# Four transformer layers on one core: setup reordered and partly moved into the first mixer, and the order of weight and modulation loads at the end of two up projections

## What is computed

```python
def first_block(x, ...):
    h = x
    for l in range(2):
        n = rms_norm(h, attn_norm[l])
        h = h + (hybrid_mixer(n, ...) if l == 0 else diff_mixer(n, ...))
        h = h + conv_glu_ffn(rms_norm(h, ffn_norm[l]), ffn_w_up[l], ffn_conv_w[l], ffn_conv_b[l], ffn_w_down[l])
    return rms_norm(h, final_norm)

def second_block(x, c, ctx, c_ctx, ada_w, ada_b, ...):
    for l in range(2):
        mod_l = split(silu(c) @ ada_w[l] + ada_b[l], 6)       # six rows of 1024 that modulate the tokens
        mod_c = split(silu(c_ctx) @ ada_w[l] + ada_b[l], 6)   # and six for the 256 context tokens
        ...                                                   # mixer and feed-forward, modulated and gated
```

## Time and profile before

| what | us |
|---|---|
| three timed executions | 2000.79, 2011.51 (median), 2018.67 |
| the profiled execution, own time | 1996.9 |
| its span, first to last instruction | 1995.1 |
| PE busy in the span | 1800.3 (90%) |
| mean granted TensorE clock | 0.948 of full speed |
| POOL busy | 935.9 (47%) |
| ACT busy | 878.3 (44%) |
| DVE busy | 721.8 (36%) |

### The profile page before, as it was taken

The page is one execution under the profiler, slowest core; times in us unless marked ns, Lnnn a source line. Parts: engine busy times, 40 slices in busy tenths (PEclk is TensorE's granted clock), DMA queues, the critical chain, the costliest instruction groups (busy, mean ns, idle before and its releaser), DMA issues.

```text
span 1995.1 us, 25840 instructions
## 1 busy us (share of the span) xinstructions
PE 1800.3 (90%) x10191; PEld 1453.6 (73%) x10191; DVE 721.8 (36%) x1591; ACT 878.3 (44%) x1541; POOL 935.9 (47%) x408
## 2 busy tenths in 40 slices
PE   2898999989879989798888998999999798889998
PEld 2666887776568878687554577888878686759986
DVE  2244232235432222337266524443401253344431
ACT  3455543435554433342334534444432255456652
POOL 2654674766346657343203023444444161137876
PEclk9999999999889999898885898999999999999999
DMA  4434998444249984232100022333323431125654
GB/s 168 150 97 137 301 306 297 162 150 136 66 147 307 305 296 154 80 100 70 64 1 1 1 63 66 104 98 92 106 74 105 105 106 43 43 85 153 186 171 146
DMA packets 257258, 261.36 MB, mean 131 GB/s; under 512 B 11107, under 2 KB 201667, under 8 KB 250867
## 3 DMA queue, kind: packets, MB, share of 16 engines
q1 hardware_dynamic: 256019, 255.10, 40.4%
q10 hardware_dynamic: 1120, 4.63, 0.6%
HBM read 258.66 MB, written 1.05 MB: 130 GB/s over the span
## 4 chain that ended last, share of the span: by engine, by line
PE 77%; DVE 8%; ACT 5%; DMA 4%; issue 2%; SPq 1%; POOL 1%; DVEq 0%; ACTq 0%
PE bank L341 21%; PE bank L342 20%; PE bank L343 20%; PE bank L1371 2%; PE bank L710 2%; PE bank L1022 2%; PE bank L733 2%; ACT weights_high L328 2%; DMA weights<-in_ffn_w_down 1%; ACT work L1140 1%; PE bank L992 1%; PE bank L1722 1%; PE bank L396 1%; PE bank L718 1%; SPq L2460 1%
## 5 line engine op out<-in xcount | busy, mean ns | idle before, releaser
L335 POOL TENSOR_TENSOR weights_low<-weights,weights_high 128x1024 fp32r<-128x1024 f32 (+1 forms) x388 | 917.3, 2381 | 954.4 <-ACT weights_high L328 954.1
L328 ACT ACTIVATE weights_high<-weights 128x1024 fp32r<-128x1024 f32 (+1 forms) x388 | 400.8, 1045 | 485.4 <-PE bank L343 143.1
L341 PE MATMUL bank<-normed_features_high,weights_high 128*128 128x256 f32 (+1 forms) x1408 | 444.6, 316 | 13.4 <-DVE normed_features_low L447 6.7
L342 PE MATMUL bank<-normed_features_high,weights_low 128*128 128x256 f32 (+1 forms) x1408 | 439.1, 312 | 0.0
L343 PE MATMUL bank<-normed_features_low,weights_high 128*128 128x256 f32 (+1 forms) x1408 | 438.7, 312 | 0.0
L341 PEld LDWEIGHTS bank<-normed_features_high,weights_high 128*128 128x128 f32 x1408 | 271.8, 193 | 65.6 <-issue 34.5
L341 PE MATMUL bank<-weights_high,normed_features_high 128*128 128x512 f32 (+4 forms) x752 | 291.5, 388 | 26.4 <-DVE normed_features_low L488 9.2
L342 PEld LDWEIGHTS bank<-normed_features_high,weights_low 128*128 128x128 f32 x1408 | 272.0, 193 | 13.8
L343 PEld LDWEIGHTS bank<-normed_features_low,weights_high 128*128 128x128 f32 x1408 | 271.8, 193 | 14.0
L343 PE MATMUL bank<-weights_low,normed_features_high 128*128 128x512 f32 (+4 forms) x752 | 276.4, 368 | 0.0
L342 PE MATMUL bank<-weights_high,normed_features_low 128*128 128x512 f32 (+4 forms) x752 | 276.3, 367 | 0.0
(11 more groups left out here) (289 smaller groups left out, 2026.2 us busy)
## 6 DMA issues: line engine op xcount, KB each, us to landing
work<-in_ada_w SPq DMA_DIRECT2D x48, 1024.0 KB, 8.0
weights<-in_ffn_w_up SPq DMA_DIRECT2D x44, 1024.0 KB, 6.3
weights<-in_ffn_up SPq DMA_DIRECT2D x44, 1024.0 KB, 6.0
weights<-in_ffn_w_down SPq DMA_DIRECT2D x20, 1024.0 KB, 5.1
weights<-in_ffn_down SPq DMA_DIRECT2D x20, 1024.0 KB, 5.0
weights<-in_diff_w_qkv SPq DMA_DIRECT2D x12, 1024.0 KB, 5.1
weights<-in_hyb_w_in SPq DMA_DIRECT2D x11, 1024.0 KB, 5.3
weights<-in_odd_w_in SPq DMA_DIRECT2D x9, 1024.0 KB, 5.3
```

Of the source, the lines that this page charges most:

```text
L328: A.eng.activation(high(whigh[:, m % HIGHS, :]), raw(wslot[:, u % SLOTS, :]), ACT.Copy).then_inc(scalar_done, A.one(("A", "high", m)))
L335: G.eng.tensor_tensor(raw(wlow[:, u % SLOTS, :]), raw(wslot[:, u % SLOTS, :]), high(whigh[:, m % HIGHS, :]).bitcast(F32), ALU.subtract).th ...
L341: T.eng.matmul(out_, lh, rh, start=first, stop=False)
L342: T.eng.matmul(out_, ll, rh, start=False, stop=False)
```

## The change

**Setup.** ACT issues the identity alone (64 KB) and the tokens `x`. SP issues weight slot 0, the gains of the first norm, weight slots 1 and 2, then everything else (25 small loads, the rest of `con` among them) and last the context tokens. A new first phase (`first_T`, `first_V`, `first_A`) turns the unscaled tokens, turns the first gains, sets the small constants, loads the square-root table, and computes the squares of the two token tiles. The first norm now has the form of `front_T`, `front_V` and `front_A`; the high parts of the first four halves are made between its features. The rest of the setup goes into the mixer: `setup_T` into cut 1 behind its second half, `setup_V` behind DVE's reads of cut 0, `setup_lambda_V` and `setup_A` behind cut 2. In `setup_A` stand an Exp, a Silu, a copy and the four squares of the context tiles.

**End of the up projections of block one.** The list `issue` now has tiles 20 and 21, the first down weights, tile 22, the second, tile 23, the third. `down_T` waits only for the first modulation rows; it uses banks 7 and 4 for the left half, the modulation columns are turned in the right half before its ninth chunk, and DVE adds the first two parts of the residual ahead of the modulation columns.

```diff
-                    issue.extend(("ada", first + n) for n in ([0, 1] if f == 2 else [f - 1] if f < FC - 1 else range(f - 1, ADA_N)))
+                    issue.extend(("ada", first + n) for n in ([0, 1] if f == 2 else [f - 1] if f < FC - 1 else [f - 1, f]))
-        def add_down_halves(ph, w):
+        def add_down_halves(ph, w, ada=()):
             begin(ph)
+            left = list(ada)
...
                     issue.append(("weights", len(stream) - 1))
+                    if left:
+                        issue.append(("ada", left.pop(0)))
...
-        add_down_halves("1.0 ffn down", io["ffn_w_down"][0])
+        add_down_halves("1.0 ffn down", io["ffn_w_down"][0], [ADA_N - 2, ADA_N - 1])
...
         def front_T(T, ph, x_ph):
 
-            turn_x_T(T, ph, x_ph, 1)
+            if x_ph != "setup":
+                turn_x_T(T, ph, x_ph, 1)
...
-                if k % 4 == 3:
+                if x_ph == "setup" and k in (0, 2, 4, 6):
+                    ahead(A, first_half[next_ph] + 1 + k // 2)
+                if x_ph != "setup" and k % 4 == 3:
                     ahead(A, first_half[next_ph] + HIGHS - 1 + k // 4)
...
-        DOWN_BANKS = {"1.0 ffn down": (2, 3, 0, 1), "1.1 ffn down": (2, 3, 0, 1), "2.0 ffn down": (4, 5, 6, 7, 0, 1, 2, 3), "2.1 ffn down": (0, 1, 6, 7)}
+        DOWN_BANKS = {"1.0 ffn down": (7, 4, 0, 1), "1.1 ffn down": (7, 4, 0, 1), "2.0 ffn down": (4, 5, 6, 7, 0, 1, 2, 3), "2.1 ffn down": (0, 1, 6, 7)}
...
-            last = FC - 3 if n > SEQ or up in WITH_ADA else FC - 2
-            T.eng.wait_ge(vector_done, done("V", up, "low", last))
+            if up in WITH_ADA:
+                T.eng.wait_ge(vector_done, done("V", up, "rows", 0))
...
-                    if half == 0 and f0 == 12 and middle is not None:
+                    if half == 1 and f0 == 8 and middle is not None:
                         middle(T)
...
+        def first_T(T):
+            T.eng.wait_ge(ident_in, 16)
+            T.eng.wait_ge(x_in, 16)
+            for half in range(2):
+                for j, t in enumerate(LAT):
+                    for k in range(4 * half, 4 * half + 4):
+                        i = T.eng.transpose(turned_k(k)[:, j * P:(j + 1) * P], xt[:, t, k * P:(k + 1) * P], ident)
+            i.then_inc(tensor_done, T.one(("T", "1.0 norm", "turned")))
+            T.eng.wait_ge(first_in, 16)
+            T.eng.transpose(psum[0][:, 0:16], vrows[0:16, :], const("ident", 0, 16, slice(0, 16))).then_inc(tensor_done, T.one(("T", "setup", "gains")))
...
+        def first_A(A):
+            A.eng.wait_ge(vector_done, done("V", "setup", "eps"))
+            A.eng.activation(stat[:, 32:33], lam[:, 6:7], ACT.Sqrt).then_inc(scalar_done, A.one())
+            A.eng.wait_ge(x_in, 16)
+            for t in LAT:
...
         def setup_A(A):
-            A.eng.wait_ge(x_in, 16 * 2)
...
+            A.eng.wait_ge(vector_done, done("V", "setup", "cols"))
             A.eng.activation(lam[:, 2:4], lam[:, 0:2], ACT.Exp).then_inc(scalar_done, A.one(("A", "setup", "exps")))
...
+            A.eng.wait_ge(ctx_in, 16)
+            for t in CTX:
+                for half in range(2):
...
-              between={(1, 2, 1): [fox_T]}, after_V={1: [fox_V]}, after_A={1: [fox_A]}, following="1.0 norm2")
+              between={(1, 1, 1): [setup_T], (1, 2, 1): [fox_T]}, after_V={0: [setup_V], 1: [fox_V], 2: [setup_lambda_V]}, after_A={1: [fox_A], 2: [setup_A]}, mixed="setup", following="1.0 norm2")
...
-                if what == "weights" and u == 2:
-
-                    for dst, src in loads[N_LOADS // 3:]:
-                        sp.dma_start(dst, src).then_inc(loaded, 16)
...
+                if u == 0:
+                    sp.dma_start(vrows[0:16, :], rows(io["attn_norm"].rearrange("a n -> (a n)"))).then_inc(first_in, 16)
+                if u == SLOTS - 1:
+                    for dst, src in loads:
+                        sp.dma_start(dst, src).then_inc(loaded, 16)
+                    sp.dma_start(xt[:, 0:2, :], io["ctx_2"][0].rearrange("(t p) d -> p t d", p=P)).then_inc(ctx_in, 16)
```

73 lines of the change are left out of this document (35 added, 38 removed).

## The result

| | before | changed |
|---|---|---|
| median of five timed runs, us | 2006.53 (2000.79 to 2018.67) | 1990.12 (1989.35 to 1990.46) |
| ratio of the changed kernel to before | | 0.9909, 95% interval 0.9886 to 0.9932 |
| profiled execution, us (span, mean granted clock) | 1996.9 (1995.1, 0.948) | 1989.65 (1987.9, 0.942) |
| PE's first product, us | 42.56 | 21.86 |
| fourth weight slot issued, us | 50.68 | 37.89 |

The change brings 16.4 us between the medians, where 28.4 were forecast, and 7.2 us between the two profiled executions. Two different things are missing: some 10 us are missing in the first 38 us of the changed kernel, and the profiled execution of before turns out to be a quick one of its program.

The account below looks back on a forecast made before the run. PE, carrying 77% of the chain, was taken to bound the kernel. Start and mixer (23.2 - 1.0 - 1.5 = 20.7 us) plus transitions (7.7) gave 28.4, so 2011.5 - 28.4 = 1983.1 us; range 1966 to 1999.

Parts of the forecast that it names:

- Beside them PE turns the tokens: Start: tokens land at 7.9 us, PE transposes them beside ACT's squares until 11.6, first product at 19.2.
- Cut 0 needs two halves ... so I keep 8.1.: First mix: cut 0 takes 8.1 us as before, its features being ready, so slot 0 is free at 27.3.
- SP must also be there by then.: Start: SP's queue, with ten more issues, is through at 25 or 26 us; mixer anchored at 27.5, saving 23.2.
- The rival of SP's queue: Start: small loads ahead of the fourth weight slot make PE wait in cut 1; slower, chance 0.05.
- The mixer, 1.0 for the transposes and 1.5 for `setup_A`: Mixer: setup work moved there costs the path 1.0 us for seven small transposes and 1.5 for ACT's `setup_A`.
- the longer price weighed in the prediction: ACT's table loads: a skill page adds a drain of about 1.38 us per switch, making `setup_A` 9.4 us; not used.
- The transitions, 2.4 + 2.3 + 3.0 = 7.7: Block one, up to down: 2.4 and 2.3 us from shorter waits in two layers, 1.5 each from regained clock.
- I take the saving over to the median unchanged.: Saving summed on the profiled execution, 1996.9 us, is subtracted whole from the timed median, 2011.51.
- nothing at the transitions: Block one, up to down: PE swaps one wait for another, clock falls the same; saves 20.7, time 1990.8, chance 0.13.
- 20.7 us for the start: Start and mixer together: 23.2 us saved at the anchor, less 1.0 and 1.5 charged in the mixer.
- ACT's new work is on the path: Mixer: all 6.6 us of `setup_A` delay PE, plus 1.7 at half clock; saves 16, time 1995.5, chance 0.12.

Follow-up runs that it names:

- experiment 11: Changed kernel with features in PSUM, bias loads early, gains turned ahead of tokens, two high parts moved, weight slots 1 and 2 behind nine small loads; 1981.45 us.
- experiment 3: Changed kernel with the first norm's features written to two PSUM banks instead of SBUF; 1983.64 us, ratio 0.9866.
- experiment 4: Changed kernel with ACT making the high parts of the first four weight halves before the features; 1982.5 us, ratio 0.987.
- 9: Changed kernel with first four high parts ahead of the features, features in PSUM, bias loads early, context squares early; 1981.62 us, ratio 0.9855.
- 12: Kernel of experiment 11 with both remaining modulation tiles of each block-one layer behind the first down weights; 1971.59 us, ratio 0.9805.
- experiment 2: Kernel before with only the new step from up to down projection in block one, old setup kept; 2001.87 us, ratio 0.9963.
- experiment 1: Changed kernel with the step from up to down projection in block one as before, so only the new setup; 1990.28 us, ratio 0.9908.

## Why the forecast was near and its sum was not

The time, 1990.1, lies in the range (1966 to 1999) and 7.0 us above the forecast of 1983.1. Point by point:

- **"Beside them PE turns the tokens", the tokens at 7.9, the first product at 19.2.** Right in kind, 2.7 us late. The tokens landed at 9.6 (8.4 us from issue, not 6.6; experiment 11 excludes weight slots 1 and 2 as the reason, which stays open). Then ACT waited 1.31 us, until 13.91, for a small operation that stands on DVE behind the turned gains, which PE turned last, at 13.31; the sum had the roots wait for the squares alone.
- **"Cut 0 needs two halves ... so I keep 8.1."** This is the step that failed, with its premise that the features "will be ready now". It took 16.0 us, 4.5 of them waits for DVE's low parts. The sum asked which engine makes each operand, and not whether two engines can work at once: the change moved POOL's subtractions beside DVE's, and each DVE subtraction with two SBUF inputs waited for one of POOL's. With the cause taken away, cut 0 took 7.4 us (experiment 3) and 8.9 (experiment 4), around the 8.1. So the term was right for a kernel without the collision, and 7.9 us were missing.
- **"SP must also be there by then."** Right: SP was through at 21.1, earlier than the 25 or 26 forecast. The rival of SP's queue can be dropped; it came true only in experiments 9, 11 and 12, where the bias loads were put there.
- **The mixer, 1.0 for the transposes and 1.5 for `setup_A`.** The 12.8 us at the fourth slot were 12.4 at the first slot of `hyb_w_out`, near the mixer's end (132.46 before, 120.02 changed): 0.4 against the 2.5 charged. Another 1.5 went between there and `ffn_w_up`, 38.6 us before and 40.1 in the changed kernel; but the second profile of before took 40.1 too, and all fourteen lie at 38.4 to 38.7 or at 40.0 to 40.2. In the 5 us that begin 15 us into this part the granted clock was 1.00 in the first profile of before and 0.74 in the changed kernel. `setup_A` took 6.3 us, forecast 6.6; ACT's rows of its head stand below. Its two table loads took 1.28 us each, the next activation begins 0.01 us behind each, and the first load begins 0.02 us behind the activations ahead of it (59.11 and 3.88 are 62.99). So the longer price weighed in the prediction is not seen here either.

```profile
59.11 3.88 ACT L334 ACTIVATE weights_high<-weights 128x1024 fp32r<-128x1024 f32 x4
63.01 1.28 ACT L1932 ACT_TABLE_LOAD   x1
64.30 0.20 ACT L1932 ACTIVATE lam<-lam 128x2 f32<-128x2 f32 x1
64.53 1.28 ACT L1933 ACT_TABLE_LOAD   x1
65.82 0.22 ACT L1933 ACTIVATE st<-veccol 128x16 f32<-128x16 f32 x1
```

- **The transitions, 2.4 + 2.3 + 3.0 = 7.7.** Measured 6.0 in the changed kernel and 8.6 alone, and some 4 over all profiles (experiment 2), so the term was rather too large. The mechanism is the one named: the wait for DVE is exchanged for one for tile 23 behind the second down weights. The sum charged 2.8 us for the megabyte ahead of it; taking that megabyte away brought 5.2 us in the first layer and 2.3 in the second (each from the layer's first up slot to the first slot of the projection that follows; between experiments 11 and 12 the same edit brought 3.0 and 3.9), with the clock that comes with it.
- **"I take the saving over to the median unchanged."** This held better than what the two profiles show. The profiled pair is only 7.2 us apart, because the profile of before is a quick execution: a second one took 2007.6, against which the changed kernel is 19.7 us faster. At the entry to block two the gain is 17.0 or 21.0 us by the two profiles, and by the medians it is 16.4 to 20.3.

The rival "nothing at the transitions" gave this very time, 1990.8, from 20.7 us for the start, of which 11 to 12 arrived, and from no gain at the transitions, which experiment 2 excludes for block one (by experiment 1 most of that gain is lost again in block two, with one more slow round of its recurrent stage). "ACT's new work is on the path" (1995.5) falls with the changed kernel itself: between the fourth slot and `ffn_w_up` 1.8 us are lost, not the 9.3 that this rival adds up. That the forecast is only 7.0 us off has a part of luck: the sum was 12.0 too high against the medians, 10.4 of it at the fourth slot (37.89 where 27.5 was forecast), and 5.0 came back only since the kernel before measured 2006.5 in five runs and not the 2011.5 of three.

## What to carry to other kernels

When an edit makes two engines work at the same time that used to take turns, look at what they share and not only at who waits for whom: here a VectorE subtraction with two SBUF inputs waited until GpSimd's was through (2.07 to 2.41 us instead of 0.42), and with one operand in PSUM it did not. Price a DMA that many wait for by what stands ahead of it in its queue; changing the order of two issues brought as much here as a rewritten transition. And profile the kernel before twice when the sum is made against its profile: two executions of one program lay 12.5 us apart.

## What the hardware showed that was not expected

- DVE's 128x256 subtraction took 0.41 to 0.43 us alone, and 2.07 to 2.41 beside POOL; a 128x128 product 0.28 and 2.50. POOL's own subtraction of 128x1024 was hardly slower for it (2.42 us each in the pair at 19.46, 2.36 in experiment 3).
- In one execution (setup alone), with the same waits, one round of the recurrent stage took 17.2 us and the next 13.9, at a granted clock of 0.70 and 0.88, and whole executions of one program differed by up to 22 us, with the mean clock between 0.940 and 0.949.
- 22 more squares on ACT ahead of the first norm put the fourth slot 15.5 us later, and the medians lie 15.6 apart: nothing behind it hid any of the delay.
